# One core, two transformer blocks: all eight expert chunks' first products ahead of the second ones, and a layer norm's sum moved to GpSimd

## The reference, cut to what matters

```python
def peer_ffn(z, peer_wq, keys1, keys2, peer_u, peer_v):   # first block
    q = (z @ peer_wq); s1 = q1 @ keys1; s2 = q2 @ keys2    # 8 heads
    ... # top 16 of 128 each, top 16 of their 256 sums -> 128 experts a token, of 16384
    gate = softmax(top_s)
    act = gelu(einsum('chkd,cd->chk', take(peer_u, expert), z))
    return einsum('chk,chkd->cd', gate * act, take(peer_v, expert))

def second_block(...):
    proj = rmsnorm_2(x) @ w_in + b_in           # q, k, v, glu_a, glu_b, gate_sb, gate_cv
    o_sb = stick_breaking_attention(q, k, v) @ w_sb_out
    u = glu_a * sigmoid(glu_b)                  # 1024 channels
    u = causal_depthwise_conv(u, w_dw, b_dw)    # 31 taps
    u = silu(layernorm(u))                      # mean and variance over the 1024 channels
    o_cv = u @ w_conv_out
    x = x + rmsnorm_2((sigmoid(gate_sb) * o_sb + sigmoid(gate_cv) * o_cv) @ w_o)
    ... # then the MLP
```

## Time and profile before

| what | value |
|---|---|
| median of 3 runs | 3244.15 us (3241.38 to 3247.28) |
| profiled execution, its time | 3243.67 us |
| profiled execution, its span (first to last instruction) | 3241.7 us |
| PE busy | 3087.3 us (95%) |
| DVE, ACT, POOL busy | 2084.5 us (64%), 1622.9 us (50%), 901.3 us (28%) |
| mean granted TensorE clock | 0.979 of full speed |
| DMA | 628 MB, mean 194 GB/s |

### The profile page before, as it was taken

How to read it: one execution, slowest core, us unless ns; L and a number is a source line. 1 busy time by engine, 2 the same in 40 slices (tenths; PEclk the granted TensorE clock), 3 DMA queues, 4 the chain that set the end, 5 groups by cost and what they waited for, 6 DMA issues and landing times.

```text
span 3241.7 us, 45915 instructions
## 1 busy us (share of the span) xinstructions
PE 3087.3 (95%) x17740; PEld 2697.4 (83%) x17740; DVE 2084.5 (64%) x3021; ACT 1622.9 (50%) x2415; POOL 901.3 (28%) x779
## 2 busy tenths in 40 slices
PE   8999999994099999999999999999999999999999
PEld 7888888884088888888888888888888888888887
DVE  7957975551076666465555569989775865555564
ACT  6654554541054444454545665665657544444444
POOL 0023288888832222131312320000151100000003
PEclk9999999997599999999999999999999999999999
DMA  6568888995277766666676665555666566666664
GB/s 241 168 203 281 285 190 201 214 214 112 0 253 240 242 218 215 190 189 216 191 215 189 190 187 182 169 179 179 180 191 189 175 184 190 191 189 189 191 190 139
DMA packets 222937, 628.02 MB, mean 194 GB/s; under 512 B 55936, under 2 KB 78848, under 8 KB 220032
## 3 DMA queue, kind: packets, MB, share of 16 engines
q1 hardware_dynamic: 157824, 572.59, 57.6%
q10 hardware_dynamic: 28032, 52.35, 4.5%
q0 software_dynamic: 36864, 0.15, 2.8%
HBM read 599.70 MB, written 25.30 MB: 193 GB/s over the span
## 4 chain that ended last, share of the span: by engine, by line
PE 71%; POOL 13%; DVE 8%; issue 5%; ACT 1%; DMA 1%; POOLq 0%; ACTq 0%; DVEq 0%
PE G L457 47%; PE G L461 23%; POOL g_scratch L1685 12%; DVE lo L1054 4%; DVE CV L1399 1%; DVE tS L1064 1%; DVE tS L1060 1%; ACT hi L703 1%; POOL X L1605 0%; POOL acc L1610 0%; PE M L536 0%; DMA raw<-in_pu 0%; ACT tQ L732 0%; DMA col<-in_cols 0%; PE M L550 0%
## 5 line engine op out<-in xcount | busy, mean ns | idle before, releaser
L457 PE MATMUL G<-ZA,hi 128*128 128x512 f32 x5104 | 1775.4, 396 | 138.8 <-ACT hi L703 122.7
L1054 DVE TENSOR_TENSOR lo<-raw,hi 128x1024 fp32r<-128x1024 f32 x1088 | 1374.7, 1284 | 263.8 <-ACT hi L703 263.2
L461 PE MATMUL G<-ZA,lo 128*128 128x256 f32 x5120 | 1394.8, 279 | 0.5 <-DVE lo L1054 0.5
L457 PE MATMUL G<-ZB,hi 128*128 128x512 f32 x3568 | 1235.1, 394 | 4.0 <-DVE ZB L1387 2.8
L457 PEld LDWEIGHTS G<-ZA,hi 128*128 128x128 f32 x5104 | 946.3, 188 | 343.7 <-ACT hi L703 123.1
L703 ACT ACTIVATE hi<-raw 128x1024 fp32r<-128x1024 f32 x1088 | 1112.9, 1051 | 114.9 <-DMA raw<-in_pv 61.6
L461 PE MATMUL G<-ZB,lo 128*128 128x256 f32 x3584 | 986.3, 277 | 0.0
L461 PEld LDWEIGHTS G<-ZA,lo 128*128 128x128 f32 x5120 | 968.3, 189 | 19.8 <-DVE lo L1054 1.0
L457 PEld LDWEIGHTS G<-ZB,hi 128*128 128x128 f32 x3568 | 666.1, 188 | 156.4 <-issue 3.1
L710 ACT ACTIVATE tA<-G 128x256 f32<-128x256 f32 x558 | 212.3, 381 | 1110.0 <-PE G L461 971.7
L461 PEld LDWEIGHTS G<-ZB,lo 128*128 128x128 f32 x3584 | 673.3, 188 | 3.8
(11 more groups left out here) (300 smaller groups left out, 1147.1 us busy)
## 6 DMA issues: line engine op xcount, KB each, us to landing
raw<-in_pu SPq DMA_DIRECT2D x256, 512.0 KB, 4.3
raw<-in_pv SPq DMA_DIRECT2D x256, 512.0 KB, 3.9
raw<-in_w_in SPq DMA_DIRECT2D x192, 512.0 KB, 3.6
raw<-in_w_up SPq DMA_DIRECT2D x128, 512.0 KB, 3.6
raw<-in_w_down SPq DMA_DIRECT2D x128, 512.0 KB, 3.6
raw<-in_w_out SPq DMA_DIRECT2D x32, 512.0 KB, 3.6
raw<-in_wq SPq DMA_DIRECT2D x32, 512.0 KB, 4.5
g_scratch<-zero ACTq DMA_DIRECT2D x16, 1024.0 KB, 6.3
```

Source lines behind the costliest of these rows:

```text
L457: pe.matmul(G[:, 0:512], w, Z[:, k, :], start=first, stop=False, skip_group_check=True)
L461: m = pe.matmul(G[:, 0:256], lo[POS[u][p] % NRAW][:, k % 8, :], weights(u, p)[1][:, k, 0:256], start=False, stop=last, skip_group_check=True)
L1054: dve.tensor_tensor(lo[r][:, :, :], raw[r][:, :].rearrange("p (k n) -> p k n", k=8), hi[w][:, :, :].bitcast(F32), ALU.subtract).then_inc(s ...
```

## The change

`KEPT` becomes 8. All eight chunks do their 16 first-product units ahead of any second one (units 56 to 183), then the eight chunks' second products follow (184 to 311). Chunks 2 to 7, six instead of three, write their gelus to `h_scratch` and come back by `load_h`; all eight are gated by `gate_kept` in 128x1024 pieces on POOL, and the scale of chunks 5 to 7 goes from POOL to DVE (`SCALE_V` follows from VB[0]). The stage order of the units, the weights' order on SP's queue with it, and the place of the first `load_g` (VB[0] - 8, now 176) follow from the tables. In the second block five taps a unit instead of four are given out in units 356 to 360, five stand at 370 and the last four at 371; the sum over channel blocks goes from DVE's reduce to seven adds on POOL (four at 352, one each at 362, 367 and 371); the sum of squares goes from one reduce to three adds on DVE. Unit M0 + 5 = 421 joins `PHASED`.

```diff
-KEPT = 5
+KEPT = 8
@@
-PHASED = [19, OT + 1, VB[0] + 2] + UB[KEPT:] + [v + 1 for v in VB[1:]] + [MG, YO + 1, M0 + 3, M0 + 17, M0 + 19] + [
+PHASED = [19, OT + 1, VB[0] + 2] + UB[KEPT:] + [v + 1 for v in VB[1:]] + [MG, YO + 1, M0 + 3, M0 + 5, M0 + 17, M0 + 19] + [
@@
+SUM_AT = {SG: (1, 2, 3, 4), SG + 10: (5,), SG + 15: (6,), SG + 19: (7,)}
+TAPS_FIVE = range(SG + 4, SG + 9)
@@ TensorE
-                    total(2, R1, None, (s_lns, 1)).then_inc(s_mean, 1)
+                    total(2, R1, None, (s_lns, 7)).then_inc(s_mean, 1)
-                    total(3, acc[0], None, (s_lnt, 1)).then_inc(s_mean, 1)
+                    total(3, acc[0], None, (s_lnt, 3)).then_inc(s_mean, 1)
@@ DVE
-                    n = min(4 if AT0[0] <= u < SG + 12 else 5, TAPS * DW_READY[u] - taps)
+                    n = min(4 if AT0[0] <= u < SG + 12 and u not in TAPS_FIVE else 5, TAPS * DW_READY[u] - taps)
@@
-                if u == SG + 18:
-                    depthwise(taps, 1000)
+                if u in (SG + 18, SG + 19):
+                    depthwise(taps, 5 if u == SG + 18 else 1000)
+                    taps += 5
@@
-                if u == SG + 19:
-                    dve.wait_ge(s_dw, 8 * TAPS)
-                    dve.tensor_reduce(R1[:, :], CV[:, :, :].rearrange("p k t -> p t k"), AX.X, ALU.add).then_inc(s_lns, 1)
@@
-                    dve.tensor_reduce(acc[0][:, :], O[:, :, :].rearrange("p k t -> p t k"), AX.X, ALU.add).then_inc(s_lnt, 1)
+                    dve.tensor_tensor(O[:, 0:4, :], O[:, 0:4, :], O[:, 4:8, :], ALU.add).then_inc(s_lnt, 1)
+                    dve.wait_ge(s_lnt, 1)
+                    dve.tensor_tensor(O[:, 0:2, :], O[:, 0:2, :], O[:, 2:4, :], ALU.add).then_inc(s_lnt, 1)
+                    dve.wait_ge(s_lnt, 2)
+                    dve.tensor_tensor(acc[0][:, :], O[:, 0, :], O[:, 1, :], ALU.add).then_inc(s_lnt, 1)
@@ POOL
-                    pool.wait_ge(s_gm2, 16 * (8 - KEPT))
+                    pool.wait_ge(s_gta, 4 * KEPT)
@@
+                for j in SUM_AT.get(u, ()):
+                    pool.wait_ge(s_dw, TAPS * (j + 1))
+                    if j > 1:
+                        pool.wait_ge(s_lns, j - 1)
+                    pool.tensor_tensor(R1[:, :], CV[:, 0, :] if j == 1 else R1[:, :], CV[:, j, :], ALU.add).then_inc(s_lns, 1)
```

## The result

The changed kernel takes 3109.01 us (median of 4 runs, 3108.27 to 3109.39) against 3243.29 us for the kernel before (4 runs, 3241.38 to 3247.28): a ratio of 0.9584, with a 95% interval of 0.9568 to 0.9601. The profiled execution took 3109.39 us, its span is 3107.5 us, 134.2 less than before.

What follows compares the result with a forecast made beforehand. TensorE, busy for 95% of the span, was taken to bound the kernel. Gains of 126.1 + 2.7 + 0 + 4.1 = 132.9 us off the profiled 3243.67 gave 3110.8, forecast as 3111 us, range 3106 to 3120.

Steps and rivals of the forecast that it cites:

- The scatter's stall: TensorE's wait for ACT's `hi` behind POOL's scatter, plus slow restart, vanishes with KEPT = 8: 126.1 us gained.
- The start of the second products: TensorE's wait for `ZB` there goes, with gates early and gating pieces spread over units 178 to 181: 2.7 us gained.
- The rest of the experts: Chunks 5 to 7 get more spills, loads, large gating pieces and DVE scales: costed at nothing.
- (b): Rival: chunk boundaries leak, TensorE waits 3.2 us at each of three and at V0: 3123 us, chance 0.06.
- (d): Rival: slower than before, U units of chunks 2 to 7 run at the spills' pace: 3299 us, chance 0.01.
- (c): Rival: scatter slows by over a quarter and is still waited for, half the stall stays: 3174 us, chance 0.02.
- The layer norm: At the mean, the reduce leaves DVE's path and TensorE waits 0.5 us: 4.1 us gained of 4.6.
- the row's two ends of 0 and 1.5: Before the mean, POOL's adds for blocks 5 and 6 push DVE by 0 to 0.74 us each.
- (a): Rival: the mean's wait of 3 us comes back and the clock falls: 3115 us, chance 0.10.
- The price of 0 for the squares' three adds: Sum of squares: three adds on DVE are shorter than a reduce, no TensorE wait hangs on them: nothing.
- without a fall of the clock: At the mean, the clock stays up after TensorE's short wait, as after the 2.8 us wait at 924.

Runs made afterwards that it cites:

- e4: The changed kernel with KEPT = 6 and POOL's old wait on s_gm2: 3154.93 us.
- e12: The changed kernel with POOL held by a semaphore until the end of unit 97 before the scatter's first issue: 3148.68 us.
- e11: The changed kernel with POOL held by a semaphore until the end of unit 85 before the scatter's first issue: 3108.37 us.
- e3: The changed kernel with KEPT = 7 and POOL's old wait on s_gm2: 3108.98 us.
- e7: The changed kernel with POOL's seven adds replaced by the old reduce on DVE, the taps still spread: 3111.84 us.
- e8: The changed kernel with the channel sum as three adds on DVE after the last tap and nothing on POOL: 3108.62 us.
- e9: The changed kernel with eight more adds on POOL, results unused, before the sum's last one: 3115.07 us.
- e2: The changed kernel with KEPT back at 5 and POOL's old wait, so only taps, sums and unit 421 are changed: 3240.02 us.
- e10: The changed kernel with five taps in seven units (354 to 360) instead of five, leaving two taps for unit 371: 3108.49 us.

## Why the prediction was right, and where not

**The scatter's stall, 126.1 us**: right, term and cause. The pairs of matmuls are all there, the first `load_g` is issued at 1018.7 (predicted 1016), the scatter's last issue at 889.5 (888), and e4 and e12 bring back 38 and 29 us of wait when the cover is taken away. e11 and e12 keep all eight chunks and move only the scatter, so it is the cover, and not the new order of units, that counts.

**The start of the second products, 2.7 of at most 3.2**: it brought all 3.2. The cause was right, the lateness behind the stall, but the picture of how it goes away was wrong in two points. The gates are not in SBUF long before: they landed only at about 1035, 25 us before the first V unit (1060.64), as in the kernel before (899.13 and 924.47). And the four gating pieces do not stand one beside each of units 178 to 181 but back to back (12.28 us), because nothing on POOL ties them to the units. The burst ended 11.2 us before ACT began the parts of `ZB` in the kernel before (911.0, 922.26) and ends 10.4 us before it now (1047.6, 1057.97), so its place against those parts does not tell the two kernels apart. What differs is where ACT and DVE stand against TensorE. Behind the stall they had units 128 to 135 to catch up on while TensorE went on at unit 131, and DVE was busy for 28.9 us of the 30 from 900 to 930; now ACT is ahead and waits for TensorE, and DVE takes the same burst out of its idle time (4.1 us busy in the ten from 1020). That the stand-still, and not the burst alone, makes the wait is shown by e11 (scatter late, burst, no stall: no wait) against e12 (stall of 28.6: wait of 3.8).

**The rest of the experts, nothing**: right. The V units have their full count at a DMA share of 0.70, and e3 shows that the eighth kept chunk costs nothing that can be seen. Rivals (b) and (d) had nothing behind them: spills landed in at most 8.8 us, where (d) needs 28. Nor had (c): the scatter took 481 us against 479.

**The layer norm, 4.1 us**: it brought 4.2, with a wait of 0.58 where I took 0.5. Its parts come out of e7 and e8: without adds on POOL the last tap ends at 2131.9, 1.2 us before TensorE asks (2133.1), as worked out (2263.1 against 2264.25). With them it ends at 2133.7 against 2134.0: POOL's adds pushed the taps by 0.9 us. That lies between the row's two ends of 0 and 1.5, and the rule of the Trainium skill (SBUF — State Buffer, two separate sides), that a DVE instruction with two SBUF inputs and a reading GpSimd instruction exclude each other, had spoken for the upper one.

Rival (a), a wait of 3 us with a fall of the clock, did not come, but e7 and e9 show how near it lies: 2 us more of wait would have done it.

The trace agrees with the rule for taps (0.84 us beside an add, up to 1.06 in e9, 0.48 alone), and joins, which read PSUM, kept their 0.42 us. POOL was held up too: three of its first adds took 4.10 us, 1.37 each, where the last took 0.72. But an add cost DVE less than its whole length (0.3 to 0.6 us of 0.74 in e9); what makes the difference is not shown. The price of 0 for the squares' three adds stands: their matmul has no wait in either trace.

The ground for 'without a fall of the clock' was weak, one wait in one trace; the last section has waits of that length with a fall behind them. It did no harm, because 0.58 us is far shorter.

**Sum**: 132.9 forecast, 134.2 by the spans; 3111 us forecast, 3109.0 measured. Of the 1.3 us between forecast and spans, 0.5 is the start of the second products and 0.7 is not placed. Unit 421 in `PHASED` was not tried alone; e2 has it in, and its 4.3 us are the mean's.

## What to carry to other kernels

A serial job on a side engine costs nothing once the main engine has enough work that does not need it: count units until the first consumer asks and compare with the job's end, both read from one trace. Past that point more cover brings nothing, as seven chunks against eight show. A place in an engine's program is no time: an engine without waits runs ahead to whatever stands next, so what is to be spread must be held by a semaphore. And before work is moved to GpSimd, where it must be priced with what it blocks on VectorE, try a shorter form of it in its old place: here three adds on VectorE did as well as seven on GpSimd.

## What was not expected of the hardware

The granted clock after a short wait of TensorE went neither by the wait's length nor by its place. The wait of 2.79 us at unit 416 is the same in every trace. Behind it the clock fell to 0.50 (1.2 GHz) for 3 to 7 us in thirteen of the fourteen, the kernel before's among them, and stayed at 1.00 only in the changed kernel's. Before, the wait and a window behind it, then the changed kernel:

```profile
2512.93 0.47 PE L457 MATMUL G<-ZA,hi 128*128 128x512 f32 x1 [2.79 <-DVE ZA L1197]
...
2514.00:2516.00 2.00, 2.00 (x8) 0.50 0.00 0
```

```profile
2378.70 0.47 PE L461 MATMUL G<-ZA,hi 128*128 128x512 f32 x1 [2.79 <-DVE ZA L1201]
...
2380.00:2382.00 2.00, 1.33 (x6) 1.00 0.00 0
```

At the start of the second products a wait of 3.10 us (e2) and one of 3.79 (e12) were followed by a fall, while 2.81 (before) and 3.42 (e4) were not. The windows behind it in e2 and e4:

```profile
926.00:928.00 2.00, 2.00 (x8) 0.50 0.00 0
```

```profile
928.00:930.00 2.00, 2.00 (x14) 1.00 0.00 0
```

At the mean 2.55 (e7), 3.01 (before) and 4.58 us (e9) were, 0.58 and 1.31 (e8) were not. So a wait of 2.5 to 3.8 us may cost the clock in one execution and not in another with the same code at that place; what decides was not tried and stays open. No wait of up to 1.31 us had a fall behind it in these traces, between 100 and 3100 us. The price differs too. At the mean it was 1.6 us. At unit 416 the changed kernel's TensorE waits again for `ZA` just behind (0.8 us), and the 20 us from the wait's start hold 44 pairs with the fall (before) against 45 without (the changed kernel), and 41 in e2 and in e10. One trace is therefore no ground for saying that a wait of this length leaves the clock alone.
